# The last stage of a three-layer fp32 kernel with an expert layer: some expert rows added by VectorE, the v gathers' lag changed, and the per-block tail cut into finer pieces

## The reference

```python
def peer_ffn(h, w_q, sub_keys, u, v):          # 8 heads, 16 picks each: 128 experts per token
    ...
    top_s, pos = lax.top_k(cand, K)
    idx = jnp.take_along_axis(cand_idx, pos, axis=-1)
    g = jax.nn.softmax(top_s, axis=-1)
    def one_block(args):                        # a block of 128 tokens
        xb, ib, gb = args
        ue = jnp.take(u, ib, axis=0)            # u, v: 16384 x 1024
        a = jnp.einsum('thkd,td->thk', ue, xb)
        w = jax.nn.gelu(a) * gb
        ve = jnp.take(v, ib, axis=0)
        return jnp.einsum('thk,thkd->td', w, ve)
...
        x = x + peer_ffn(rmsnorm(x, norm_ffn), peer_wq, peer_subkeys, peer_u, peer_v)
        g_ple = jax.nn.sigmoid(rmsnorm(x, norm_ple) @ ple_gate)
        x = x + g_ple * (p @ ple_proj)
```

## Time and profile before

| | us |
|---|---|
| median of 3 runs (3266.94 to 3280.2) | 3270.82 |
| the profiled execution's own time | 3281.61 |
| its span | 3279.8 |
| PE busy in the span | 2818.6 (86%) |
| DVE busy | 1861.9 (57%) |
| POOL busy | 1321.6 (40%) |
| ACT busy | 666.9 (20%) |

### The profile page before, as it was taken

One profiled execution on the slowest core, in us unless ns is written; L12 is line 12 of the kernel. 1 busy time (PEld: TensorE's weight loads), 2 busy tenths in 40 slices (PEclk: granted clock), 3 DMA queues, 4 the chain that ended last, 5 costly groups with the idle time before them and its releaser, 6 DMA issues.

```text
span 3279.8 us, 27043 instructions
## 1 busy us (share of the span) xinstructions
PE 2818.6 (86%) x7972; PEld 1353.8 (41%) x7972; DVE 1861.9 (57%) x4204; ACT 666.9 (20%) x1588; POOL 1321.6 (40%) x1123
## 2 busy tenths in 40 slices
PE   9999999998889899879899789977777787668778
PEld 4455445454554444555545433422232232223223
DVE  4989402057750321368835766667777666666640
ACT  1114301022320112434421111111121111112111
POOL 3720000000000000024301777777777777777772
PEclk9999999999999999889999999999999999999999
DMA  4221122120112112000023999999999999999994
GB/s 179 77 103 52 64 77 82 72 77 26 45 46 77 61 71 80 0 23 29 26 103 135 327 376 370 380 410 409 398 394 377 371 373 382 351 374 360 395 408 158
DMA packets 160891, 665.85 MB, mean 203 GB/s; under 512 B 17793, under 2 KB 18177, under 8 KB 153729
## 3 DMA queue, kind: packets, MB, share of 16 engines
q0 software_dynamic: 147456, 536.94, 42.9%
q1 hardware_dynamic: 11456, 117.43, 9.6%
q10 hardware_dynamic: 1856, 10.00, 0.8%
HBM read 662.19 MB, written 2.10 MB: 203 GB/s over the span
## 4 chain that ended last, share of the span: by engine, by line
PE 53%; POOL 19%; issue 9%; DVE 9%; DMA 7%; ACT 3%; DVEq 0%; ACTq 0%; SPq 0%; POOLq 0%
PE ps L506 13%; POOL G L1539 9%; PE ps L972 8%; PE ps L672 6%; POOL H L1552 5%; POOL XT L1552 4%; PE ps L609 4%; PE ps L847 4%; DMA H<-peer_v,C 3%; PE ps L810 3%; DMA G<-peer_u,C 3%; PE ps L868 2%; PE ps L1042 2%; PE ps L933 2%; DMA XT<-peer_v,C 1%
## 5 line engine op out<-in xcount | busy, mean ns | idle before, releaser
L2224 DVE CUSTOM_DVE_ANT_0 G<-G,H 128x1024 f32<-128x1024 f32 x512 | 627.8, 1226 | 427.8 <-DMA G<-peer_u,C 423.2
L972 PE MATMUL ps<-H,MK 128*128 128x512 f32 x1216 | 593.1, 617 | 172.3 <-DMA H<-peer_v,C 120.1
L1539 POOL DMA_INDIRECT G<-peer_u,C x512 | 529.3, 1034 | 303.7 <-issue 152.5
L506 PE MATMUL ps<-XT,W 128*128 128x512 f32 (+1 forms) x1344 | 543.4, 553 | 9.0 <-issue 6.6
L972 PE MATMUL ps<-XT,MK 128*128 128x512 f32 x832 | 407.1, 621 | 127.8 <-DMA XT<-peer_v,C 102.3
L972 PEld LDWEIGHTS ps<-H,MK 128*128 128x128 f32 x1216 | 220.3, 194 | 517.7 <-issue 381.3
L1552 POOL DMA_INDIRECT H<-peer_v,C x304 | 349.1, 1148 | 111.2 <-issue 56.5
L506 PEld LDWEIGHTS ps<-XT,W 128*128 128x128 f32 x1344 | 254.3, 190 | 294.8 <-issue 286.7
L1500 POOL COPY PR<-H 128x256 f32<-128x256 f32 x4 | 1.4, 390 | 785.5 <-DVE H L1895 785.5
L972 PEld LDWEIGHTS ps<-XT,MK 128*128 128x128 f32 x832 | 150.2, 194 | 378.2 <-issue 274.1
L1403 ACT ACTIVATE MK<-C 128x128 f32<-128x128 f32 x512 | 178.0, 393 | 444.8 <-PE ps L972 332.6
(11 more groups left out here) (295 smaller groups left out, 3141.0 us busy)
## 6 DMA issues: line engine op xcount, KB each, us to landing
W<-wstream SPq DMA_DIRECT2D x51, 2048.0 KB, 8.0
G<-peer_u,C POOLq DMA_INDIRECT x512, 6.4
H<-peer_v,C POOLq DMA_INDIRECT x304, 6.4
XT<-peer_v,C POOLq DMA_INDIRECT x208, 6.5
XT<-xT SPq DMA_DIRECT2D x8, 256.0 KB, 5.3
W<-wstream SPq DMA_DIRECT2D x8, 256.0 KB, 6.0
X<-x SPq DMA_DIRECT2D x1, 2048.0 KB, 18.9
SIG<-rows ACTq DMA_DIRECT2D x4, 512.0 KB, 6.4
```

Source lines behind the costliest of these rows:

```text
L506: mm = pe.matmul(b[:, 0:rhs[k].shape[-1]], w[:, k, m * P:(m + 1) * P], rhs[k], start=(k == 0), stop=(k == KD - 1))
L972: mm = pe.matmul(ps[2 * b + half][:, :], DG[v % DIAG_RING], VB[at][:, half * T:(half + 1) * T], start=(n == FIRST[b] and k == 0), stop=(n ...
L1539: pool.indirect_dma_start(UB[u % U_RING], None, peer_u, bass.IndirectOffsetOnAxis(ap=IDX[:, u:u + 1], axis=0)).then_inc(u_loaded[u % U_RIN ...
L2224: dve.tensor_tensor_reduce(out=rows_u, in0=rows_u, in1=tm(H, 0, D, group(n)[0]), scale=1.0, scalar=0.0, op0=ALU.mult, op1=ALU.add, accum_o ...
```

## The change

- `by_vector(v)` picks rows of v that DVE adds itself (`add_row`: X += weight x row, one scalar_tensor_tensor over 1024 columns, no diagonal, no matmul). These are v = 5, 13, ..., 93, that is 12 of the first 96 rows, each after the dot of u = `v_over(v)` + 1 = v + 26 and its routing step; and ten rows of the last 30, v = 482, 485, ..., 509, after all dots.
- A gather whose buffer held such a row waits for `v_added` in place of `v_done`. PE's and ACT's rows are counted by `by_tensor`.
- `v_issued`: v is exactly 24 behind u up to u = 120, then seven v for eight u until it is 32 behind (u = 184), and 32 behind from there.
- `weigh(n)` comes before the diagonal of row 16n - 6 (n below 10) or 16n - 8, for the last group row 488.
- The block's tail: PE transposes X itself and the factor 1/rms goes into the sigmoid's `scale`; ACT copies one half and DVE the other; the 16 matmuls of the gate go in 8 pieces of two between rows (`ple_gate(b, j)`); the projection of blocks 1 to 3 goes ahead, 12 rows before the block's last, into the banks of the block before; output is added and stored by halves (two stores of 256 KB per block).

```diff
@@ -45,6 +45,8 @@
 DIAG_RING = 8
 V_BEHIND = 24
 V_EARLY = 96
+V_SLOW = 120
+V_LATE = PICKS - 30
 DIAG_AHEAD = 6
 A_RING = 8
 GELU_C = float(np.sqrt(2 / np.pi))
@@ -133,7 +135,9 @@
 def v_issued(u):
-    return max(0, (u - V_BEHIND) * (PICKS - 32) // (PICKS - V_BEHIND))
+    if u <= V_SLOW:
+        return max(0, u - V_BEHIND)
+    return max(V_SLOW - V_BEHIND + (u - V_SLOW) * 7 // 8, u - 2 * PEER_K)
 def v_over(v):
...
@@ -155,9 +159,31 @@
     return v - V_RING if v >= V_EARLY + V_RING else None
+def by_vector(v):
+    return v % 8 == 5 if v < V_EARLY else v >= V_LATE and v % 3 == 2
+def vector_rows(v):
+    return sum(by_vector(a) for a in range(v + 1))
+def by_tensor(v):
+    return sum(not by_vector(a) for a in range(v + 1))
 def weighed_at(n):
     return PEER_K * (n + 1)
+def weighed_row(n):
+    return PEER_K * n - (8 if n >= 10 else 6)
 def program(nc, x, xT, mem, wstream, fmvec, rows, norm_rows, consts, levels, subkeys, pT, proj, peer_u, peer_v, out):
...
@@ -961,15 +997,17 @@
                 block_transposes("xT_f", RES, b)
             def expert_row(v):
+                if by_vector(v):
+                    return
                 n, k = v // PEER_K, v % PEER_K
                 b = group(n)[0]
                 if v == 0:
                     pe.wait_ge(tail_free, made)
                 at, uses = v_place(v)
-                pe.wait_ge(diag_full, v + 1)
+                pe.wait_ge(diag_full, by_tensor(v))
                 pe.wait_ge(v_loaded[at], 16 * uses)
                 for half in range(2):
-                    mm = pe.matmul(ps[2 * b + half][:, :], DG[v % DIAG_RING], VB[at][:, half * T:(half + 1) * T],
+                    mm = pe.matmul(ps[2 * b + half][:, :], DG[by_tensor(v - 1) % DIAG_RING], VB[at][:, half * T:(half + 1) * T],
                                    start=(n == FIRST[b] and k == 0), stop=(n == LAST[b] and k == PEER_K - 1),
                                    skip_group_check=True)
                 mm.then_inc(v_done, 1)
...
@@ -1027,40 +1065,48 @@
             pe.wait_ge(bank_free, POS["end"] + 4)
             def ple_transposes(b):
-                pe.wait_ge(xn_ready, NB + 1 + b)
                 for half in range(2):
+                    pe.wait_ge(ple_x, 2 * b + half + 1)
                     for k in range(4):
-                        c0 = b * D + (4 * half + k) * P
-                        mm = pe.transpose(ps[2 * b + half][:, k * P:(k + 1) * P], RES[:, c0:c0 + P], ident)
+                        c0 = (4 * half + k) * P
+                        mm = pe.transpose(ps[2 * b + half][:, k * P:(k + 1) * P], X[:, b, c0:c0 + P], ident)
                     mm.then_inc(ple_xT_full, 1)
-            def ple_gate(b):
-                for n in range(2):
-                    w = slot(SLOTS["ple"], n).rearrange("p (k n) -> p k n", k=KD)
-                    pe.wait_ge(ple_xT_copied, 2 * b + 2)
-                    for k in range(KD):
-                        mm = pe.matmul(ps[2 * b + n][:, :], Y[:, b * 2048 + k * P:b * 2048 + (k + 1) * P], w[:, k, :],
-                                       start=(k == 0), stop=(k == KD - 1))
+            def ple_gate(b, j):
+                n = j // 4
+                w = slot(SLOTS["ple"], n).rearrange("p (k n) -> p k n", k=KD)
+                if j == 0:
+                    pe.wait_ge(ple_xT_copied, b + 1)
+                if j == 2:
+                    pe.wait_ge(ple_xT_scaled, b + 1)
+                for k in range(2 * (j % 4), 2 * (j % 4) + 2):
+                    mm = pe.matmul(ps[2 * b + n][:, :], Y[:, b * 2048 + k * P:b * 2048 + (k + 1) * P], w[:, k, :],
+                                   start=(k == 0), stop=(k == KD - 1), skip_group_check=True)
+                if j % 4 == 3:
                     mm.then_inc(ple_full, 1)
             def ple_proj(b):
                 w = PROJ.rearrange("p (k n) -> p k n", k=2)
                 pe.wait_ge(loaded_p, 16)
                 pe.wait_ge(loaded_proj, 16)
+                if b > 0:
+                    pe.wait_ge(y_ready, 2 * b)
                 for n in range(2):
-                    pe.wait_ge(ple_gate_ready, 2 * b + n + 1)
+                    if b == 0:
+                        pe.wait_ge(ple_gate_ready, n + 1)
                     for k in range(2):
-                        mm = pe.matmul(ps[2 * b + n][:, :], PLE_P[:, k, b * P:(b + 1) * P], w[:, k, n * T:(n + 1) * T],
+                        mm = pe.matmul(ple_bank(b, n)[:, :], PLE_P[:, k, b * P:(b + 1) * P], w[:, k, n * T:(n + 1) * T],
                                        start=(k == 0), stop=(k == 1))
                     mm.then_inc(ple_proj_full, 1)
-            for v in range(V_EARLY, PICKS + 36):
+            for v in range(V_EARLY, PICKS + 40):
                 for b in range(NB):
-                    if v == LAST_V[b] + 22:
+                    if v == LAST_V[b] + 18:
                         ple_transposes(b)
-                    if v == LAST_V[b] + 26:
-                        ple_gate(b)
-                    if v == LAST_V[b] + 32:
+                    if LAST_V[b] + 24 <= v < LAST_V[b] + 32:
+                        ple_gate(b, v - LAST_V[b] - 24)
+                    if v == (LAST_V[b] - 12 if b > 0 else LAST_V[b] + 36):
                         ple_proj(b)
                 if v < PICKS:
                     expert_row(v)
...
@@ -1395,45 +1441,47 @@
             def diagonal(v):
+                if by_vector(v):
+                    return
+                at = by_tensor(v - 1)
                 n = v // PEER_K
                 if v % PEER_K == 0:
                     act.wait_ge(weights, n + 1)
-                if v >= DIAG_RING:
-                    act.wait_ge(v_done, v - DIAG_RING + 1)
-                act.activation(DG[v % DIAG_RING], ident, ACT.Copy, scale=GW[:, v:v + 1]).then_inc(diag_full, 1)
+                if at >= DIAG_RING:
...
                 for b in range(NB):
-                    if v == LAST_V[b] + 18:
+                    if v == LAST_V[b] + 25:
+                        ple_copies(b)
+                    if v == LAST_V[b] + 31:
                         ple_root(b)
-                    if v == LAST_V[b] + 29:
-                        ple_copies(b)
-                    if v == LAST_V[b] + 33:
+                    if v == LAST_V[b] + 37:
                         ple_sigmoid(b)
             def diagonals(first, end):
                 for v in range(first, end):
...
@@ -1546,8 +1594,11 @@
                     pool.wait_ge(tail_free, 24)
                 if v == V_EARLY + 4:
                     pool.wait_ge(bank_free, POS["end"] + 4)
-                if v_before(v) is not None:
-                    pool.wait_ge(v_done, v_before(v) + 1)
+                last = v_before(v)
+                if last is not None and by_vector(last):
+                    pool.wait_ge(v_added, vector_rows(last))
+                elif last is not None:
+                    pool.wait_ge(v_done, by_tensor(last))
                 at = v_place(v)[0]
...
+            def add_row(v):
+                at, uses = v_place(v)
+                b = group(v // PEER_K)[0]
+                dve.wait_ge(v_loaded[at], 16 * uses)
+                dve.wait_ge(weights, v // PEER_K + 1)
+                dve.scalar_tensor_tensor(X[:, b, :], VB[at], GW[:, v:v + 1], X[:, b, :], ALU.mult, ALU.add
+                                         ).then_inc(v_added, 1)
+                dve.wait_ge(v_added, vector_rows(v))
             def ple_sum(b):
-                dve.wait_ge(v_done, LAST_V[b] + 1)
+                dve.wait_ge(v_done, by_tensor(LAST_V[b]))
                 for half in range(2):
                     cols = slice(half * T, (half + 1) * T)
-                    ch.link(dve.tensor_tensor(X[:, b, cols], X[:, b, cols], ps[2 * b + half][:, :], ALU.add))
+                    dve.tensor_tensor(X[:, b, cols], X[:, b, cols], ps[2 * b + half][:, :], ALU.add).then_inc(ple_x, 1)
...
+            def ple_scale(b):
+                dve.wait_ge(ple_xT_full, 2 * b + 2)
+                for m in range(4, KD):
+                    ins = dve.tensor_scalar(Y[:, b * 2048 + m * P:b * 2048 + (m + 1) * P],
+                                            ps[2 * b + 1][:, (m - 4) * P:(m - 3) * P], fm("ple_g", m), None, ALU.mult)
+                ins.then_inc(ple_xT_scaled, 1)
+                dve.wait_ge(ple_x, 2 * b + 2)
...
-            def ple_scale(b):
+            def ple_factor(b):
                 dve.wait_ge(std_ready, 20 + b)
-                ch.link(dve.reciprocal(ST[:, b:b + 1], ST[:, 4 + b:5 + b]))
-                dve.tensor_scalar(RES[:, b * D:(b + 1) * D], X[:, b, :], ST[:, b:b + 1], None, ALU.mult
-                                  ).then_inc(xn_ready, 1)
+                dve.reciprocal(ST[:, b:b + 1], ST[:, 4 + b:5 + b]).then_inc(ple_scale_ready, 1)
             def ple_out(b):
                 for n in range(2):
+                    cols = slice(n * T, (n + 1) * T)
                     gate = Y[:, b * 2048 + D + n * T:b * 2048 + D + (n + 1) * T]
```

(28 more changed lines are left out.)

27 lines of the change are left out of this document (17 added, 10 removed).

## The result

The change makes the kernel slower: 3319.22 us (median of 4 runs, 3315.14 to 3323.38) against 3272.09 us for the kernel before, run beside it (4 runs, 3266.94 to 3280.2). The ratio is 1.0134, 95% interval 1.0105 to 1.0164. The forecast was 3303 us, in a range of 3255 to 3335.

The account below looks back on a forecast made before the run. POOL's 1024 gathers were taken to bound the last stage. Early rows +50, lag and weighing 0, tails +3 and end -20 gave +33 us: 3314 us by the profiled execution, 3303 us against the median, range 3255 to 3335.

Parts of the forecast that it names:

- The early rows, +50: First 96 rows of v: twelve DVE additions hold buffers and stall POOL, 66 - 10 - 6 = 50 us, bounds 33 to 75.
- What comes back: Early rows: set against 66 us of stalls, at most 10 us of PE waits and 6 us of gather lengthening.
- The addition at 1.28 us: Early rows: DVE's addition of one row of 1024 columns takes 1.28 us, extrapolated from 742 ns for 512 columns.
- Lag and weighing, 0: Later gathers: the lag of v and earlier weighing change nothing, 0 us, bounds -51 to +36 by which rhythm holds.
- after it the windows are as before: Sign that the forecast is right: behind the first 96 rows, the last stage's windows stay unchanged.
- The rival of the rhythm that turns: After 2429 us: landing takes 7 us or more, dots no longer lie across gathers; -35 us, 3235 us, chance 0.11.
- The tails, +3: Tails of blocks 0 to 2: PE is 1 us too late for the buffers three times; +3 us, bounds 0 and 12.
- Six rows at 0.7 us lost each bring PE to 23, 1 us too late: Tails: PE reaches 23 us behind a row's gather, where eight buffers allow 22, so 1 us late at three blocks.
- The end, -20: Behind the last dot: last row of v 10 us sooner and block 3's tail 23 against 33 us, together -20 us.
- From 3314 to 3303: Final step: 10.8 us taken off because the profiled execution of before lay that far over its three runs' median.
- some 2 us more: The end: PE's 22 rows and block 3's projection between them add some 2 us to the last row's time.
- stalls mostly swallowed: Early rows: all 23 us of lengthening come back, plus a third of the late 51; -1 us, 3269 us, chance 0.17.

Follow-up runs that it names:

- experiment 1: The changed kernel without DVE's twelve early rows (PE adds them again), all else as changed: 3253.8 us, ratio 0.995 to the kernel before.
- experiment 4: The kernel before with only the twelve early rows on DVE added: 3336.8 us, ratio 1.0206 to the kernel before.
- experiment 8: The changed kernel without early rows, with the weighing (exponentials) at its old place: 3321.18 us on another chip, ratio 0.9951 to the kernel before.
- experiments 5 and 11: The changed kernel without early rows, DVE's tail copies six rows of u sooner, run on two chips: ratios 0.9925 and 0.9938 to the kernel before.
- experiments 7: The changed kernel without early rows, with DVE's routing step ahead of the dot: 3321.36 us on another chip, ratio 0.9947 to the kernel before.
- experiment 9: The changed kernel without early rows, tail copies six rows sooner, plus a small DVE search before every dot: 3289.88 us, ratio 1.0055 to the kernel before.
- experiment 10: The changed kernel without early rows, with dots over 512 of 1024 columns: 3193.29 us, ratio 0.9762 to the kernel before.
- experiment 2: The changed kernel with each early addition two rows of u sooner, behind the dot of u = v + 24: 3275.15 us, ratio 1.0019 to the kernel before.

## Why the prediction was right, and where its numbers were off

- **The bound** held: POOL's gathers set the stage. In the traces POOL's idle time beyond the gaps grew by 55 us in the early stretch and 8 in the middle, its gathers took some 5 us less, and the end took 23.7 off.
- **The early rows, +50: the stall right, the net partly luck.** Twelve waits of 61.4 us in all (forecast 66, each 5.1 us for 5.5), the real waits for PE 6 us less (forecast 10 less), lengthening 3 us less (forecast 6 less); with one gather fewer in the stretch that makes the +50. But this is the net against the kernel before. Against the same kernel without early rows (experiment 1) they cost 64 us there: 58 us of idle time and 6 us more of lengthening, not less. Put into the kernel before (experiment 4) they cost 60, with 6 us coming back. So the step that was mis-sized is "What comes back": it took 16 us off their cost, and at most 6 came back. The net still came to +50 because the stretch without them is 13 us shorter than before, which nothing in the forecast foresaw: luck. For the change without early rows my terms give -17 us, and experiment 1 measured -15: there the shorter early stretch was made up for by the middle.
- **The addition at 1.28 us: right**, 1.28 and 1.29 us in every row. It is 1.25 ns per column for 1024 columns with two sources in SBUF. The Trainium skill (Vector Engine (DVE) Microarchitecture Reference, section 7) has this operation at half throughput with two such sources, from which I had estimated 2.4 us; this trace does not bear it out.
- **Lag and weighing, 0: right in sum, by luck in its parts.** The weighing is worth nothing (experiment 8). From u = 128 to 511 the gathers took 0.7 us less in sum. But "after it the windows are as before" is false: the fast rhythm of u = 128 to 240 was lost (+19 us) and the slow one from 240 on got faster (-21 us), and I had reckoned with neither. The first happened in all ten traces that have the new lag and whole dots (1.09 to 1.15 us per gather there, against 1.02 before and 1.04 in experiment 4 with the old lag). The rival of the rhythm that turns fails on its own test: rows of u landed after 6.5 us in the middle of the changed kernel, not 7.
- **The tails, +3: under-sized**, 8.2 us at three tails. The step that failed is "Six rows at 0.7 us lost each bring PE to 23, 1 us too late": PE was 2.6 to 2.8 us too late at each. As written the sum does not close either: 15.5 and 6 x 0.7 make 19.7, and it comes to 23 only if the gate's third piece and the row behind it (3.45) are added. The mechanism was as put, since copies 6 rows sooner take the waits away (experiments 5 and 11).
- **The end, -20: right in kind, -23.7 in size.** The last row came 12.1 us sooner behind the last dot (forecast 10), the block's tail was 11.6 us shorter (forecast 10). I had given each of ten additions half a microsecond of lengthening. The nine steps of POOL that began during an addition took 0.99 to 1.17 us, so it was about 0.1 each: the row's landing sets when its addition begins, and little of it is left when the next gather begins, 0.35 us at 3252.01. The wait for PE behind block 3's projection, 2.5 us beyond the gap, is the "some 2 us more" of the forecast.
- **From 3314 to 3303: the largest error, 16 us.** By the profiled executions the forecast was 3314 and the result 3316.16. I took off 10.8 us because the profiled execution of before lay over its median. That of after lay 3 us below its own median, which makes 2 + 11 + 3 = 16. Runs of one kernel on one chip differ by up to 29 us here (3252.5 to 3281.5 for the kernel before beside experiment 1) and runs with half dots by 0.3 us. So the place of one profiled execution in that spread carries over to no other kernel; I should have widened for it, not shifted by it.

Of the other rivals: stalls mostly swallowed would have needed 23 us of lengthening to come back, and 3 did; behind six of the twelve stalls the gather began beside a dot that had been held back too (1889.10), behind eleven of twelve in experiment 4. Not settled is what sets, from one execution to the next, how many dots lie across gathers; experiments 7 and 9 moved the dots and did not control it.

## What to carry to other kernels

Work moved from one engine to another takes its place in that engine's order with it. Before such a move, follow the buffer: when must it come free, what stands ahead of its new user, and who queues behind the refill. A transfer issued in order turns one late buffer into idle time for all of them. Here POOL really waited for PE only 10 us in the early stretch, so the move could earn no more than that there, while the same move on the last rows, where every row is on the path and nothing is refilled behind it, earned 10 us. And where the runs of one kernel spread by nearly 1%, take the trace for the mechanism and the medians for the size, and carry no offset between them over.

## What was not expected of the hardware

A gather issued by POOL is lengthened only if it begins while DVE runs an instruction of a certain kind, the dot above all. In the trace of the kernel before, from 1855 to 3180 us, 482 gathers began during a dot and 212 of them took over 1.05 us, with some 120 us of lengthening; of the 467 others 7 did. How long one takes follows max(0.94, time to the dot's end + 0.81 us) to within 0.1 us for 474 of the 482, so it is as if nearly the whole gather started again behind the dot. Seven of the other eight began within 0.04 us of the dot's recorded start and took 0.94 us: there the gather seems to have come first. The rule holds as well in the other twelve traces, for 96 to 99% of such gathers. Experiment 10 halves the dots and takes 109 of 127 us of lengthening away.

Not all work of DVE does it. From the trace of the kernel before, in the tail of block 1:

```profile
2582.36 1.41 DVE L2175 TENSOR_TENSOR X<-X,ps 128x512 f32<-128x512 f32 x2
2583.12 0.94 POOL L1539 DMA_INDIRECT G<-peer_u,C  x1 [0.30 <-issue]
...
2615.18 0.75 DVE L2183 TENSOR_SCALAR H<-X,ST 128x1024 f32<-128x1024 f32 x1
2615.51 1.22 POOL L1539 DMA_INDIRECT G<-peer_u,C  x1 [0.31 <-issue]
...
2661.97 1.22 DVE L2191 TENSOR_TENSOR X<-X,Y 128x1024 f32<-128x1024 f32 x1
2662.31 1.70 POOL L1552 DMA_INDIRECT XT<-peer_v,C  x1 [0.31 <-issue]
```

An addition with one source in PSUM (L2175, and L2190 likewise) left all six gathers that began during it at 0.93 or 0.94 us. An addition with both sources in SBUF (L2191), and the scaling of one SBUF source by a factor (L2183), lengthened the gathers that began during them; these ended 0.8 us behind DVE's instruction. The seven long gathers that met no dot all began during L2191, L2183 or the mean square over X (L1843). The early additions of experiment 2 do it too, and of the 209 gathers that began during the added search of experiment 9, with one source in SBUF, 197 took 0.93 or 0.94 us. So it is neither any work of DVE nor the transfers' own queue.

The Trainium skill describes a lock of this kind (SBUF — State Buffer, "SBUF: two separate sides"): VectorE and GpSimd share a pair of ports, an instruction with two SBUF inputs may hold it (against a GpSimd instruction that reads SBUF), and whoever starts first keeps it. That the dots, L2191 and the early additions lengthen a gather, that the additions from PSUM do not, and that a gather that came first is not touched agree with it; that it is this lock is argued here, not shown. The same page has a transfer blocked until about 115 ns behind the VectorE instruction's end. Here POOL's step ended 0.81 us behind it, and the trace does not show when within that time its work went on.

And less lengthening did not bring the whole gain: 109 us of it went in experiment 10, but the kernel was only some 60 us faster than experiment 1 by their ratios, since POOL then waited for PE, 80.7 us in 104 waits from 2200 to 3190 us, 49 of them beyond the gaps.
